# Products of halves for the gate and the squares, later distance tables, and GpSimd's low halves in pieces of 256 columns, in a hybrid decoder layer

## The chip, the cores and the metric

The kernel runs on one core of a Trainium2 chip. The metric is the device time of one execution in microseconds; the median of three runs is given for the kernel before, and beside it one profiled execution whose trace is read here. Engines are named TensorE (PE in the rows, PEld for its weight loads), VectorE (DVE), ScalarE (ACT), GpSimd (POOL) and SyncE (SP).

## The reference

One residual layer over 512 tokens of width 1024, all in float32. What matters, cut down:

```python
h = rmsnorm(x, norm_mix_pre)
p_rwkv, p_conv, p_attn, p_gate = split(h @ w_in)          # 1024 -> 8704 columns
# branch A, RWKV-7 time mixing, 8 heads of 64 (inputs shifted by a token and mixed)
w_log = -softplus(-(w0 + tanh(wl) @ w_up)) - 0.5
a = sigmoid(a0 + al @ a_up)
g = sigmoid(gl) @ g_up                                    # the gate product
kk = k * k_k;  kk = kk * rsqrt(max(sum(kk * kk), 1e-12))  # the sum of squares, by head
state = state * w + (state @ -kk) * (kk * a) + v * k;  y = state @ r
y = groupnorm(y) * ln_w + ln_b + sum(r * k * r_k) * v;  y_a = y * g
# branch B, gated convolution of 3 taps: y_b = b * conv3(c * xc)
# branch C, attention: 3 groups of 4 heads, (window, dilation) = (128, 1), (512, 4), (2048, 16),
# scores + ALiBi distance bias, masked, softmax, groups merged by their denominators: y_c
merged = sum_i sigmoid(gate_i) * (y_i @ w_branch_i)
x = x + rmsnorm(merged @ w_out, norm_mix_post)
x = x + rmsnorm((silu(gate) * up) @ w_ffn_out, norm_ffn_post)    # gate, up = split(rmsnorm(x) @ w_ffn_in)
```

## The kernel before

**Halves.** Nearly every matrix product is made as three products of fp32r operands. ScalarE copies a raw fp32 tile to an fp32r one (the high half), another engine subtracts it from the raw tile (the low half), and TensorE adds high x high, high x low and low x high in PSUM (`three`, L2144). Weights come in slots of 128 x 2048 raw elements, two buffers by turns: SyncE loads `w_raw`, ScalarE makes `w_hi` (`high`, L886), GpSimd makes `w_lo` (`low`, L736, four parts of 512 columns, each announced by itself on `lo_ready`), TensorE waits for each part before it uses it (`part_ready`).

**Stages, in order of the profile's time.** To 87 us the projection columns of the recurrence. From 87 to 424 us four turns `rwkv(T)` of 128 tokens each, in which TensorE fills every stretch between the recurrence's small products with products of the remaining projection (`fill`, `fill_steps`, L2278), written out by hand with a fixed count at each place. From 424 to 487 us the attention, with the last projection slots as fill (`fill_left`, L2462). Then the branch products (to 553), the output projection (to 575), the turn to the FFN input (to 590), six plain FFN slots (to 655), sixteen slots of mixed products (to 811) and the FFN output.

**Recurrence.** In each turn ScalarE takes tanh and sigmoid of the LoRA inputs for the next turn (`lora_inputs`, L997), and later squares `kk` (L1006), then sigmoid of `sig` (L1008), the copy of the gate (L1011), the square root of the sums (L1016), in turns two to four the next slot's `w_hi` (`next_high`), and the exponentials (L1021). TensorE multiplies the gate (`gate`, L2299, fp32) and the squares with a matrix of ones by head (L2316, fp32). VectorE waits for that (L1611). At the end of a turn VectorE normalises y (L1723 to L1744), multiplies by the gate (L1746), and TensorE turns the result (`turn_y`, L2420), asks for the next turn's LoRA products (L2293) and the next gate. In the first turn the turn of y comes after the gate.

**Attention.** Units u = 0 to 7 are heads: 0 to 3 of the window group, 4 to 7 of both dilated groups together. Pairs p are two units. TensorE: `turn_values` (L2472), `scores` (L2488), `turn_probs` (L2497), `outputs` (L2522). VectorE's order: `dilated_bias` (distances from GpSimd's `step_i`, L1509 to L1514, then eight bias tables, L1518), `keep_values` (L1757), `softmax_input` for pairs 0 and 1 (L1781), four low halves (L1800), and so on. For units 4 to 7 the blocks of the 16-dilated group are turned by VectorE in quarters of 32 (`turn_quarters`, L1809) and the others by TensorE. `scores(1)` waits until VectorE has read the scores of pair 0, `turn_probs(4)` until the last values are kept.

**Mixed FFN products.** For each slot s: VectorE adds blocks of raw weights (L2007, L2009, L2013, L2020), ScalarE makes high halves, GpSimd makes the low halves of two blocks at once, 1024 columns in one instruction (`b_low`, L835, and `t12_low`, L842), VectorE those of other blocks (L2025; in the first two slots L2031 too). TensorE's order is p1(s+1), q5(s+1), c12(s), u3(s), c11(s+1), u2, each of twelve products of 256 columns (L2692 to L2694); p1 waits for `b_low`, q5 for `t12_low`.

## Time and profile before

| | |
|---|---|
| median of 3 runs | 943.91 us (943.84 to 943.98) |
| the profiled execution's own time | 944.08 us |
| its span | 942.1 us |
| mean granted TensorE clock | 0.999 |
| TensorE busy | 932.1 us, 6650 products |
| VectorE busy | 647.7 us |
| ScalarE busy | 430.9 us |
| GpSimd busy | 442.9 us |

Products overlap: one with 512 columns is recorded as some 0.39 us long, but the next starts 0.23 us after it. So pitches, start to start, are read and not durations. "Idle before, releaser" names what an engine waited for; x4 with one duration are four instructions in a row, from the first's start to the last's end, which holds waits between them too, and also what an instruction itself waited after its start.

### The profile page before, as it was taken

How to read it: one execution, taken by the hardware profiler on the slowest of the kernel's cores; microseconds unless marked ns; L12 is line 12 of the kernel's file. 1: busy time of each engine (PE TensorE's matmuls, PEld its weight loads, DVE VectorE, ACT ScalarE, POOL GpSimd, SP SyncE). 2: the span in 40 equal slices, each digit the busy share in tenths (PEclk: the TensorE clock that was granted, in tenths of full speed). 3: DMA queues.
4: the chain of work that ended last, by engine and by line, in shares of the span. 5: the costliest groups of instructions: out<-in, count | busy, mean ns of one | idle time of the engine just before them, and what ended most of it. 6: DMA issues, size and time to landing. Idle time of an engine off the chain costs nothing.

```text
span 942.1 us, 16109 instructions
## 1 busy us (share of the span) xinstructions
PE 932.1 (99%) x6650; PEld 786.1 (83%) x6650; DVE 647.7 (69%) x831; ACT 430.9 (46%) x626; POOL 442.9 (47%) x328
## 2 busy tenths in 40 slices
PE   9999999999999999999999999999999999999997
PEld 7888877787887778777778888888999999988886
DVE  6777967766586756899885656988998898411114
ACT  6423515723461462336653425574556655322332
POOL 4884524344253245253245553514765565555551
PEclk9999999999999999999999999999999999999999
DMA  8323332342333265229144842286557666343312
GB/s 290 114 91 112 111 113 92 113 150 73 129 108 130 84 219 183 92 76 327 68 158 158 309 144 71 79 194 162 131 143 176 154 148 169 81 145 112 111 45 89
DMA packets 110805, 128.44 MB, mean 136 GB/s; under 512 B 3216, under 2 KB 87184, under 8 KB 110736
## 3 DMA queue, kind: packets, MB, share of 16 engines
q1 hardware_dynamic: 100224, 102.64, 33.8%
q0 software_dynamic: 2880, 10.49, 5.9%
q10 hardware_dynamic: 7632, 14.32, 4.0%
q8 instruction: 52, 0.85, 0.4%
q14 instruction: 17, 0.14, 0.1%
HBM read 100.70 MB, written 16.25 MB: 124 GB/s over the span
## 4 chain that ended last, share of the span: by engine, by line
PE 52%; issue 26%; POOL 16%; DVE 4%; ACT 1%; DMA 0%; POOLq 0%; DVEq 0%; ACTq 0%
POOL w_lo L741 15%; PE ps L2146 11%; PE ps L2147 11%; PE ps L2148 11%; PE ps L2692 5%; PE ps L2694 5%; PE ps L2693 5%; PE ps L2462 2%; PE ps L2522 1%; DVE x_ct L1527 1%; DVE bias_dil L1518 1%; PE ps L2497 0%; PE ps L2191 0%; PE ps L2488 0%; ACT p_buf L1125 0%
## 5 line engine op out<-in xcount | busy, mean ns | idle before, releaser
L741 POOL TENSOR_TENSOR w_lo<-w_raw,w_hi 128x512 fp32r<-128x512 f32 x220 | 317.6, 1473 | 377.8 <-ACT w_hi L890 377.4
L890 ACT CAST w_hi<-w_raw 128x2048 fp32r<-128x2048 f32 x55 | 105.0, 1909 | 135.4 <-PE ps L2148 110.3
L2278 PE MATMUL ps<-a_hi,w_hi 128*128 128x512 f32 x384 | 154.8, 403 | 0.0
L2278 PE MATMUL ps<-a_lo,w_hi 128*128 128x512 f32 x384 | 152.1, 396 | 0.0
L2278 PE MATMUL ps<-a_hi,w_lo 128*128 128x512 f32 x384 | 151.1, 393 | 0.0
L2278 PEld LDWEIGHTS ps<-a_hi,w_hi 128*128 128x128 f32 x384 | 72.1, 188 | 17.1 <-issue 1.0
L2278 PEld LDWEIGHTS ps<-a_lo,w_hi 128*128 128x128 f32 x384 | 72.2, 188 | 15.5 <-issue 1.0
L2278 PEld LDWEIGHTS ps<-a_hi,w_lo 128*128 128x128 f32 x384 | 72.1, 188 | 15.0 <-ACT xs L1051 0.2
L2063 DVE TENSOR_TENSOR f_lo<-f_all,f_hi 128x1024 fp32r<-128x1024 f32 x11 | 16.1, 1467 | 82.8 <-ACT f_hi L1325 82.8
L2692 PE MATMUL ps<-form_hi,w_hi 128*128 128x256 f32 x256 | 72.5, 283 | 0.0
L2694 PE MATMUL ps<-form_hi,w_lo 128*128 128x256 f32 x256 | 72.5, 283 | 0.0
L2693 PE MATMUL ps<-form_lo,w_hi 128*128 128x256 f32 x256 | 72.5, 283 | 0.0
L2146 PE MATMUL ps<-w_hi,f_hi 128*128 128x512 f32 x176 | 68.6, 390 | 0.0
L2147 PE MATMUL ps<-w_lo,f_hi 128*128 128x512 f32 x176 | 68.5, 389 | 0.0
L2148 PE MATMUL ps<-w_hi,f_lo 128*128 128x512 f32 x176 | 68.5, 389 | 0.0
L981 ACT COPY spill_buf<-ps 128x512 f32<-128x512 f32 x36 | 20.9, 585 | 72.3 <-PE ps L2278 72.0
L835 POOL TENSOR_TENSOR w_lo<-w_raw,w_hi 128x1024 fp32r<-128x1024 f32 x16 | 41.7, 2608 | 24.3 <-ACT w_hi L1253 24.3
L2146 PE MATMUL ps<-a_hi,w_hi 128*128 128x512 f32 (+1 forms) x144 | 53.0, 368 | 0.0
L2147 PE MATMUL ps<-a_lo,w_hi 128*128 128x512 f32 (+1 forms) x144 | 52.7, 366 | 0.0
L2148 PE MATMUL ps<-a_hi,w_lo 128*128 128x512 f32 (+1 forms) x144 | 52.7, 366 | 0.0
L2694 PE MATMUL ps<-form_hi,late_lo 128*128 128x256 f32 x180 | 51.0, 283 | 0.0
L2693 PE MATMUL ps<-form_lo,late_hi 128*128 128x256 f32 x180 | 51.0, 283 | 0.0
(407 smaller groups left out, 2241.6 us busy)
## 6 DMA issues: line engine op xcount, KB each, us to landing
w_raw<-w_in SPq DMA_DIRECT2D x32, 1024.0 KB, 5.2
w_raw<-w_ffn_in SPq DMA_DIRECT2D x44, 512.0 KB, 5.0
spill<-spill_buf ACTq DMA_DIRECT2D x27, 512.0 KB, 3.1
w_raw<-w_ffn_out SPq DMA_DIRECT2D x11, 1024.0 KB, 4.9
late_lo<-w_raw POOLq DMA_DIRECT2D x14, 512.0 KB, 4.6
w_raw<-w_branch SPq DMA_DIRECT2D x5, 1024.0 KB, 8.1
g_ab<-spill SPq DMA_DIRECT2D x8, 512.0 KB, 4.8
w_raw<-w_out SPq DMA_DIRECT2D x4, 1024.0 KB, 7.3
```

The lines of the kernel that those rows point to most:

```text
L741: g.tensor_tensor(w_lo[:, b, c], w_raw[:, b, c], w_hi[:, b, c].bitcast(F), ALU.subtract).then_inc(lo_ready, 1)
L835: g.tensor_tensor(w_lo[:, b, 0:2 * BLK], w_raw[:, b, 0:2 * BLK], w_hi[:, b, 0:2 * BLK].bitcast(F), ALU.subtract).then_inc(b_lo_made.sem, 1)
L890: s.copy(w_hi[:, b], w_raw[:, b]).then_inc(hi_ready, 1)
L981: s.copy(spill_buf[:, b, half], ps[:, 6 + half]).then_inc(spill_copied, 1)
L2146: t_.matmul(dst, w0, a0, start=first, stop=False)
L2147: t_.matmul(dst, w0, a1, start=False, stop=False)
L2148: return t_.matmul(dst, w1, a0, start=False, stop=last)
L2278: last = t_.matmul(ps[:, 6 + half], w[:, kt, half * P:(half + 1) * P], a, start=(kt == 0 and step == 0), stop=(kt == KT - 1 and step == 2))
L2462: last = t_.matmul(ps[:, LEFT_BANK[i]], w[:, kt, half * P:(half + 1) * P], a, start=(kt == 0 and step == 0), stop=(kt == KT - 1 and step = ...
L2692: t_.matmul(dst, hi[:, c], form_hi[f][:, k], start=first and k == 0, stop=False, skip_group_check=not first)
L2693: t_.matmul(dst, hi[:, c], form_lo[f][:, k], start=False, stop=False, skip_group_check=not first)
L2694: last = t_.matmul(dst, lo[:, c], form_hi[f][:, k], start=False, stop=k == KT // 2 - 1, skip_group_check=not first)
```

## The change

It does five things.

1. The gate product is made of halves: ScalarE copies `g_up` once and the sigmoid of each turn to fp32r, VectorE subtracts (`g_up_lo` once, `gate_low` each turn; for turns two to four ahead of the last product of the turn before), TensorE makes three fp32r products.
2. The sum of squares is made of two products of fp32r (the ones are exact): a copy on ScalarE right behind Square and ahead of the sigmoid, a subtraction on VectorE behind the additions to `sig`. In the first turn the first tile's evacuation goes ahead of the sigmoid.
3. GpSimd's low halves in `low`, `b_low` and `t12_low` are made in instructions of 256 columns. What is announced, and when, stays.
4. VectorE's attention order: it waits for the last turn of y, clears `pt_dil`, makes the distances, then four low halves, then values and softmax inputs of pairs 0 and 1, and only then the bias tables.
5. Unit 5's blocks of the 16-dilated group are turned by TensorE (four more) and copied by ScalarE (1024 columns instead of 512), and not by VectorE in quarters.

```diff
+    POOL_PIECE = 256
...
+        ON_VECTOR = (4, 6, 7)
+        def turned_blocks(u):
+            return [b for b in blocks(u // HG) if u not in ON_VECTOR or b[2] == 1]
...
+            def pieces(c0, c1):
+                return [slice(c, c + POOL_PIECE) for c in range(c0, c1, POOL_PIECE)]
             def low(n, b):
                 pool.wait_ge(hi_ready, n + 1)
                 for q in range(LO_PARTS):
-                    c = slice(q * SLOT // LO_PARTS, (q + 1) * SLOT // LO_PARTS)
-                    g.tensor_tensor(w_lo[:, b, c], w_raw[:, b, c], w_hi[:, b, c].bitcast(F), ALU.subtract).then_inc(lo_ready, 1)
+                    for c in pieces(q * SLOT // LO_PARTS, (q + 1) * SLOT // LO_PARTS):
+                        last = g.tensor_tensor(w_lo[:, b, c], w_raw[:, b, c], w_hi[:, b, c].bitcast(F), ALU.subtract)
+                    last.then_inc(lo_ready, 1)
...
             for n in range(5, N_RWKV + 2):
+                if n == N_RWKV:
+                    act.wait_ge(ups_ready, 48)
+                    s.copy(g_up_hi[:], g_up[:]).then_inc(ups_ready, 1)
                 high(n, raw_value(n), n % 2)
...
-                    s.activation(xm[:, RT - 1], xm[:, RT - 1], ACT.Sigmoid).then_inc(gate_ready.sem, 1)
+                    s.activation(xm[:, RT - 1], xm[:, RT - 1], ACT.Sigmoid).then_inc(gate_then_hi.sem, 1)
+                    act.wait_ge(gate_then_hi.sem, gate_then_hi.at(turn))
+                    s.copy(gate_hi[:], xm[:, RT - 1]).then_inc(gate_then_hi.sem, 1)
...
-                s.activation(sq[:], kk[:], ACT.Square).then_inc(sq_ready.sem, 1)
-                need(z_ready)
+                s.activation(sq[:], kk[:], ACT.Square).then_inc(sq_then_hi.sem, 1)
+                need(sq_then_hi)
+                s.copy(sq_hi[:], sq[:].rearrange("p j t -> p (j t)")).then_inc(sq_then_hi.sem, 1)
+                if T == 0:
+                    copy_tile(0)
+                need(z_then_sq_lo)
                 s.activation(sig[:], sig[:], ACT.Sigmoid).then_inc(sig_ready.sem, 1)
...
+            def gate_low(turn):
+                dve.wait_ge(gate_then_hi.sem, gate_then_hi.at(turn, 1))
+                v.tensor_tensor(gate_lo[:], xm[:, RT - 1], gate_hi[:].bitcast(F), ALU.subtract).then_inc(gate_lo_made.sem, 1)
...
+                if T == 0:
+                    dve.wait_ge(ups_ready, 49)
+                    v.tensor_tensor(g_up_lo[:], g_up[:], g_up_hi[:].bitcast(F), ALU.subtract).then_inc(ups_ready, 1)
+                    gate_low(0)
                 need(z_done)
...
+                need(sq_then_hi, 1)
+                v.tensor_tensor(sq_lo[:], sq[:].rearrange("p j t -> p (j t)"), sq_hi[:].bitcast(F),
+                                ALU.subtract).then_inc(z_then_sq_lo.sem, 1)
                 need(ssq_done)
...
                 link(v.tensor_tensor(y1[:], y1[:], y2[:], ALU.add))
+                if T < NT - 1:
+                    gate_low(T + 1)
                 need(g_ready)
...
-            dilated_bias()
+            dve.wait_ge(y_turned.sem, y_turned.at(NT - 1))
+            v.memset(pt_dil[:], 0.0).then_inc(dil_turned.sem, 1)
+            dilated_distances()
+            low_parts(0, NJ)
             keep_values(0, 4)
             softmax_input(0)
             softmax_input(1)
-            low_parts(0, NJ)
+            dilated_bias()
             keep_output(0)
-            v.memset(pt_dil[:], 0.0).then_inc(dil_turned.sem, 1)
             keep_values(2, 4)
             softmax_input(2)
             keep_output(1)
             turn_quarters(4)
-            turn_quarters(5)
...
-                    pe.wait_ge(gate_ready.sem, gate_ready.at(turn))
-                    t_.matmul(ps[:, 2], xm[:, RT - 1], g_up[:], start=True, stop=True).then_inc(g_done.sem, 1)
+                    pe.wait_ge(gate_then_hi.sem, gate_then_hi.at(turn, 1))
+                    pe.wait_ge(ups_ready, 49)
+                    t_.matmul(ps[:, 2], gate_hi[:], g_up_hi[:], start=True, stop=False)
+                    pe.wait_ge(ups_ready, 50)
+                    t_.matmul(ps[:, 2], gate_hi[:], g_up_lo[:], start=False, stop=False)
+                    pe.wait_ge(gate_lo_made.sem, gate_lo_made.base + turn + 1)
+                    t_.matmul(ps[:, 2], gate_lo[:], g_up_hi[:], start=False, stop=True).then_inc(g_done.sem, 1)
...
-                need(sq_ready)
-                t_.matmul(ps[:, 3], head_ones[:], sq[:].rearrange("p j t -> p (j t)"), start=True, stop=True).then_inc(ssq_done.sem, 1)
+                need(sq_then_hi, 1)
+                t_.matmul(ps[:, 3], head_ones[:].bitcast(R), sq_hi[:], start=True, stop=False)
+                need(z_then_sq_lo, 1)
+                t_.matmul(ps[:, 3], head_ones[:].bitcast(R), sq_lo[:], start=False, stop=True).then_inc(ssq_done.sem, 1)
```

`b_low` and `t12_low` are split in the same way, four pieces for one instruction. Semaphores are renamed where they now count two events, and a few tiles are placed anew.

## Rows read from the trace of the kernel before

**Rows 1.** The page's first part: busy us, share of the span, instructions.
```profile
PE 932.1 (99%) x6650; PEld 786.1 (83%) x6650; DVE 647.7 (69%) x831; ACT 430.9 (46%) x626; POOL 442.9 (47%) x328
```
**Rows 2.** TensorE's waits: waiting <- waited for: us in total, times, longest.
```profile
PE ps L2488 <- DVE p_buf L1781: 1.2, 1, 1.2
PE ps L2497 <- DVE proj L1757: 0.8, 1, 0.8
PE ps L2692 <- DVE up L2051: 0.4, 1, 0.4
...
PE ps L2472 <- DMA proj<-spill: 0.2, 1, 0.2
```
**Rows 3.** TensorE's timeline, third turn: start us, us, engine, line, operation, count.
```profile
248.82 1.13 PE L2299 MATMUL ps<-g_up,xm 128*128 128x512 f32 x2
249.78 0.60 PE L2305 MATMUL ps<-ident,xm 128*128 128x128 f32 x4
...
259.32 1.02 PE L2316 MATMUL ps<-sq,head_ones 128*128 128x512 f32 x2
...
260.41 0.40 PE L2278 MATMUL ps<-a_lo,w_hi 128*128 128x512 f32 x1
...
267.02 0.39 PE L2278 MATMUL ps<-a_hi,w_hi 128*128 128x512 f32 x1
267.25 0.39 PE L2278 MATMUL ps<-a_lo,w_hi 128*128 128x512 f32 x1
```
**Rows 4.** Timeline, third turn: VectorE's last product, TensorE's turn of y, ScalarE.
```profile
246.29 0.69 DVE L1746 TENSOR_TENSOR y<-y,g_tok 128x512 f32<-128x512 f32 x1
...
247.20 0.60 PE L2420 MATMUL ps<-ident,y 128*128 128x128 f32 x4
...
257.04 0.65 ACT L1006 ACTIVATE sq<-kk 128x512 f32<-128x512 f32 x1
...
259.68 1.28 ACT L1016 ACT_TABLE_LOAD   x1
261.10 0.63 ACT L1016 ACTIVATE sq<-sq 128x512 f32<-128x512 f32 x1
```
**Rows 5.** Timeline: GpSimd's low halves at three places; TensorE in the output projection.
```profile
5.12 0.73 POOL L749 TENSOR_TENSOR w_lo<-w_raw,w_hi 128x256 fp32r<-128x256 f32 x1 [4.59 <-ACT w_hi L929]
...
263.61 5.99 POOL L741 TENSOR_TENSOR w_lo<-w_raw,w_hi 128x512 fp32r<-128x512 f32 x4 [9.97 <-ACT w_hi L890]
...
564.03 5.03 POOL L741 TENSOR_TENSOR w_lo<-w_raw,w_hi 128x512 fp32r<-128x512 f32 x4 [2.58 <-ACT w_hi L890]
...
569.27 0.40 PE L2146 MATMUL ps<-w_hi,a_hi 128*128 128x512 f32 x1
```
**Rows 6.** Timeline, mixed products, second slot: GpSimd, VectorE, TensorE.
```profile
656.16 2.41 POOL L835 TENSOR_TENSOR w_lo<-w_raw,w_hi 128x1024 fp32r<-128x1024 f32 x1 [5.67 <-ACT w_hi L1253]
658.53 2.85 POOL L842 TENSOR_TENSOR w_lo<-t_second,w_hi 128x1024 fp32r<-128x1024 f32 x1
...
656.72 2.40 DVE L1971 TENSOR_TENSOR f_all<-f_all,f_silu 128x512 f32<-128x512 f32 x1 [0.45 <-ACT f_silu L1220]
659.15 3.31 DVE L2031 TENSOR_TENSOR late_lo<-w_raw,late_hi 128x1024 fp32r<-128x1024 f32 x1
...
661.97 0.28 PE L2692 MATMUL ps<-form_hi,w_hi 128*128 128x256 f32 x1
```
**Rows 7.** Timeline, end of the last turn and attention: VectorE, TensorE.
```profile
421.57 1.67 DVE L1746 TENSOR_TENSOR y<-y,g_tok 128x512 f32<-128x512 f32 x1
...
428.32 5.13 DVE L1518 SCALAR_TENSOR_TENSOR bias_dil<-step_f,ahead_f 128x128 f32<-128x128 f32 x4
...
434.29 1.29 DVE L1757 COPY proj<-ps 128x512 f32<-128x512 f32 x2
...
459.61 1.25 DVE L1809 STREAM_TRANSPOSE pt_dil<-p_buf 32x128 f32<-32x128 f32 x4 [0.18 <-ACT p_buf L1125]
...
437.75 1.79 PE L2488 MATMUL ps<-proj 64*128 64x128 f32 x16 [1.23 <-DVE p_buf L1781]
```

More of the change, by code:

```diff
@@ L834, in b_low @@
                 pool.wait_ge(b_hi_made.sem, b_hi_made.base + s + 1)
-                g.tensor_tensor(w_lo[:, b, 0:2 * BLK], w_raw[:, b, 0:2 * BLK], w_hi[:, b, 0:2 * BLK].bitcast(F),
-                                ALU.subtract).then_inc(b_lo_made.sem, 1)
+                for c in pieces(0, 2 * BLK):
+                    last = g.tensor_tensor(w_lo[:, b, c], w_raw[:, b, c], w_hi[:, b, c].bitcast(F), ALU.subtract)
+                last.then_inc(b_lo_made.sem, 1)
             def t12_low(s):
@@ L841, in t12_low @@
                 pool.wait_ge(t12_hi_made.sem, t12_hi_made.base + s + 1)
-                g.tensor_tensor(w_lo[:, b, 2 * BLK:], t12_of(s)[:], w_hi[:, b, 2 * BLK:].bitcast(F),
-                                ALU.subtract).then_inc(t12_lo_made.sem, 1)
+                for c in pieces(0, 2 * BLK):
+                    to = slice(2 * BLK + c.start, 2 * BLK + c.stop)
+                    last = g.tensor_tensor(w_lo[:, b, to], t12_of(s)[:, c], w_hi[:, b, to].bitcast(F), ALU.subtract)
+                last.then_inc(t12_lo_made.sem, 1)
             def late_low(s):
@@ L1018, in rwkv @@
                     next_high(T - 1, PER_T - 1)
[L1019 removed]
+                    evacuate(0)
                 need(sums_run)
@@ L2515, in outputs @@
                 if kind == 1:
-                    pe.wait_ge(dil_turned.sem, dil_turned.base + 2 * p - 1)
+                    pe.wait_ge(dil_turned.sem, dil_turned.base + 1 + sum(u < 2 * p + 2 for u in ON_VECTOR))
                 bl = blocks(kind)
```

57 lines of the change are left out of this document (31 added, 26 removed).

## The prediction

> **What bounds the kernel now.** I read the page's busy shares first: TensorE is busy for 932.1 of 942.1 us, VectorE and GpSimd for 69% and 47% [rows 1]. So the end is set by the sum of TensorE's instruction pitches and its few gaps. The table of waits comes second: TensorE's named waits are 1.2 us for the score tiles that VectorE reads out, 0.8 us for attention values that VectorE keeps, 0.4 us in the mixed FFN products and 0.2 us for a DMA [rows 2]. Two things can therefore move the time: what TensorE issues, and whether a producer (GpSimd's low halves, ScalarE's high halves, VectorE) that now arrives in time comes late. For the second I took, in the timeline, each producer's end beside the product that needs it.
>
> **Recurrence, products.** Per turn the gate product (L2299) and the sum of squares (L2316) are fp32 with 512 columns, each run as two instructions. Gate: from 248.82 to the next product at 249.78, 0.96 us, of which I put 0.10 down to the change of operand shape after the LoRA products, which stays (the sum of squares, without it, has 0.86). A product of halves is issued every 0.23 us (267.02 to 267.25), so three cost 0.68: 0.18 saved. Sum of squares: from 259.32 to the second fill product at 260.41 is 1.09 us, less that fill product's own 0.23, so 0.86; two products of halves cost 0.45: 0.41 saved [rows 3]. Four turns: 4 x (0.18 + 0.41) = 2.36 us. Bounds: the gate could save 0.28 in three turns (+0.3), or the two extra waits between its three products could cost 0.1 each turn (-0.4).
> The trace shows an fp32 product as two instructions. The Trainium skill, "FP8 and Floating Point Precision", section TensorE Precision Notes, speaks of four passes for true fp32; at 0.23 us a pass the saving would be 0.23 + 0.45 a turn, 2.7 us in all. The rows give less, and I go by them.
>
> **Recurrence, new work.** On VectorE the gate's low half (128x128, 0.25 to 0.3 us) stands ahead of the last product with the gate. That product ends at 246.98 and TensorE turns its result at 247.20, its normal pitch, so nearly nothing covers it [rows 4]: 0.2 us lost in turns two and three, -0.4. In the first turn TensorE asks for the gate before the turn of y, and the low half would be there about when its third product is: -0.05. Its high half follows ScalarE's sigmoid directly and is there before VectorE comes to it. The sum of squares' low half: Square starts at 257.04 and takes 0.65, the copy some 0.6 and VectorE's subtraction 0.69, to 259.1; the second product wants it at 259.5. Covered by 0.3 us.
> The copy of the squares' high half is queued ahead of sigmoid, gate copies, table load, square root and the next high half of the weights on ScalarE. In turns three and four the table load ends at 260.96 and the root starts at 261.10, so the root, the weights' high half behind it and GpSimd's low half at 263.61 slip by 0.5 us [rows 4, 5]. TensorE is 0.41 earlier there. GpSimd's four parts, 5.99 us for all, end at 265.1 to 269.6; TensorE takes the first at 267.02 [rows 3] and then one in six products, 1.36 us: 1.2 to 1.9 us in hand, 0.2 less by the weight loads that go ahead. Less 0.5, 0.41 and the 0.56 of the pieces (below) leaves nothing in the last part, but 0.95 of the 5.99 is waiting for VectorE (5.99 - 4 x 1.26), and VectorE's last two-input operation before its reciprocal moves out from under it. I take 0, with 0.5 a turn as the bad end.
>
> **GpSimd's pieces.** Free of VectorE, four parts of 512 take 5.03 us (1.26 each) and a piece of 256 alone took 0.73 (0.70 in a row, as an estimate, since operations that follow one another overlap by 0.03): a part grows by 0.14 us, a slot by 0.56, 1024 columns by 0.4 [rows 5]. What VectorE gains shows at the same place as what GpSimd loses. A VectorE operation with two SBUF inputs that meets a GpSimd one waits until that ends and then holds it off: VectorE's L1971 took 2.40 instead of 0.69 beside GpSimd's L835, and the next GpSimd operation took 2.85 instead of 2.41 [rows 6]. With pieces VectorE waits 0.7 at most, but can hold GpSimd off after each of them, by 0.45 us per 512 columns.
> The Trainium skill states such a lock (SBUF — State Buffer, section Who interferes with whom: held for the whole instruction, against a GpSimd operation that reads SBUF); the trace agrees, and by it pieces help VectorE and never GpSimd.
> Output projection: the slot whose parts GpSimd makes from 564.03 to 569.06 gives its last part just as TensorE wants it, with the weight load ahead of its product at 569.27 [rows 5]. Four parts 0.14 longer: -0.56. The other slots have 0.9 us or more in hand.
> Mixed FFN products, second set: GpSimd runs 656.16 to 658.57 and 658.53 to 661.38, and TensorE's product with this result starts at 661.97, 0.5 us in hand. In pieces: the first four end at 659.4 (wanted at 660.5). Then VectorE's L2031, 1024 columns, waiting since 658.9 instead of 659.15, takes the port for 1.0 us (now it gets it at 661.38, when GpSimd is done, and ends at 662.46) [rows 6]. Its next two operations, now at 662.7 and 663.4, come to lie beside the last four pieces: 659.4 + 1.0 + 4 x 0.70 + 2 x 0.45 = 664.1 us. So TensorE stops for 2.3 us (0.6 if the long operation stays behind GpSimd). Its gap later in these products (0.4 us of wait [rows 2], 0.56 with the pitch), behind a VectorE chain that GpSimd held up, goes: -1.75 net.
>
> **Attention.** (a) VectorE's last product with the gate in turn four, like the two before it, took 1.67 us instead of 0.69 beside GpSimd [rows 7]. In pieces each takes some 1.15, the attention loads that wait for it start 1.4 us earlier, and the DMA wait (0.2 [rows 2], 0.33 with the pitch) goes: +0.33. (b) The eight bias operations (from 428.32, 5.13 for the first four, to 434.26) leave the path to the first scores, four low halves come onto it. They start at 428.5 and each meets a piece: 4 x 1.15, to 433.0. Keeping the values and the first softmax input then take the same 3.4 us (434.29 to 437.7), to 436.4; TensorE now goes on at 437.75 after 1.23 us of wait, so it wants them at 436.5: +1.2 [rows 7]. Ends: 0 (low halves at 1.7 each) and 1.39. The bias tables then lie beside TensorE's outputs, some 2 us, needed 5 us later. (c) Without the quarters of unit 5 (1.25 us) the values are kept from 460.2, when their turn lands, not from 460.9 [rows 7]: the wait of 0.8 [rows 2], 0.94 with the pitch, shrinks by 0.74. (d) Unit 5 gives TensorE four more turns; four turns of y take up to 0.60 [rows 4], 0.44 by pitch. ScalarE's copy doubles to about 1.0, -0.08 for the outputs behind it. Sum: 0.33 + 1.2 + 0.74 - 0.44 - 0.08 = +1.75.
>
> **The sum.** 2.36 - 0.45 + 1.75 - 0.56 - 1.75 = 1.35 us gained. The profiled execution took 944.08 us (span 942.1 and 2.0 around it), 0.17 above the median of 943.91. That gives 942.7 by the profile's own time, 942.6 by the median's. I predict 942.6.
>
> **The rivals.** (1) The stop in the mixed products doesn't come: the long low half gets the port only after the last piece, or lies elsewhere. For it: the order at a boundary is seen at only a few places. Against it: VectorE had the port at the end of every GpSimd operation that it waited for. The gap at 671 goes all the same, so 2.3 us more are gained, less 0.2: 940.5. (2) The change doesn't take the wait for the first scores away, since the tables' six small operations are still ahead of the low halves and these wait for full pieces: 1.2 us less, and 0.4 to 0.7 more if the values are late too: 944.0 to 944.5. For it: GpSimd is busy there from 428.1 on. (3) Slower: in each later turn the first slot's low half comes late, behind ScalarE's new copy, since VectorE takes the port after most pieces. It decides from the point where the port is lost at two to three more boundaries than I counted: 0.45 us each, in three turns, is 1.35 per boundary; four of them cost 5.4 us: 948.0. Against it: VectorE's reciprocal, 3.4 us with one input, lies in just that stretch.
> The Trainium skill's rule on the lock, as cited above, leaves it to whoever comes first, so it excludes neither (1) nor (3).
>
> **How the numbers follow.** About 0.2% (1.9 us) is what a measurement of this kernel can tell from no change. Forecast 0.46, of which 0.10 lies below 942.0; (1) 0.25; (2) 0.17; (3) 0.12, slower. So faster 0.35, same 0.53, slower 0.12. The range takes in (1) and (2), and leaves out (3) and the outer ends of the bounds: 940.3 to 944.9.
>
> **What would show it.** In the changed kernel's trace: gate 0.7 us and sum of squares 0.45 us in TensorE's timeline; no named wait above 0.3 us for the first scores or the kept values; two gaps that are not there now, some 0.5 us at 569 and 1 to 2.5 us at 662 (less what was gained by then), both for a GpSimd low half; VectorE's 2.4 to 3.3 us operations in the mixed products down to 1.2 to 2. I am wrong if GpSimd's 256 column pieces take more than 0.75 us free of VectorE, or if a TensorE wait for a low half shows in the recurrence.

## The result

The changed kernel takes 948.96 us (median of 6 runs, 946.97 to 950.06) against 943.88 us for the kernel before in the same session (943.32 to 944.01). The ratio is 1.0051, with a 95% interval of 1.0041 to 1.0061: slower by 0.5%, where 942.6 us was forecast, with a range up to 944.9. The scatter grew as well, from 0.7 to 3.1 us. The profiled execution of the changed kernel took 947.77 us (span 946.0), 3.7 us more than the profiled one of before and 1.2 us less than its own median.

The page's first part of the changed kernel, the answer to [rows 1]:

```profile
PE 933.6 (99%) x6658; PEld 787.6 (83%) x6658; DVE 598.2 (63%) x836; ACT 436.5 (46%) x635; POOL 527.7 (56%) x644
```

VectorE is busy for 49 us less and GpSimd for 85 us more; TensorE, which sets the end, got nothing of the first. A stop is, here and below, a time in which TensorE runs no product. Its waits, the answer to [rows 2]:

```profile
PE ps L2744 <- POOL w_lo L860: 2.5, 1, 2.5
PE ps L2250 <- DVE all_ones L1450: 1.2, 1, 1.2
PE ps L2420 <- issue: 0.8, 1, 0.8
PE ps L2540 <- DVE p_buf L1825: 0.6, 1, 0.6
PE ps L2191 <- POOL w_lo L755: 0.5, 2, 0.3
PE ps L2323 <- POOL w_lo L755: 0.3, 2, 0.2
```

The first is the stop that the prediction put into the mixed FFN products. The waits for the score tiles and for the kept values shrank or went (1.2 to 0.6, 0.8 to none). New are a wait for "issue" in the recurrence's small products, and waits for GpSimd's low halves in four more places.

I then set the start of each TensorE product beside the start of the same product before. The difference between the two profiled executions changes at these places (own working from the two traces; plus is time lost):

| place | forecast | measured |
|---|---|---|
| products of halves in four turns, with the gate's low half | -1.91 | -1.60 |
| last parts of the first slot, turns three and four | 0 | +0.85 |
| stop for "issue" in the third turn | - | +1.17 |
| attention: loads -0.26, first scores -0.68, kept values -0.71, transposes +0.43 | -1.75 | -1.22 |
| output projection, one slot | +0.56 | +0.44 |
| plain FFN products: later parts +0.84, turn of x -0.25 | - | +0.59 |
| mixed products: the stop | +2.3 | +2.86 |
| mixed products: half clock behind the stop | - | +1.43 |
| mixed products: the gap ten us later goes | -0.56 | -0.56 |
| sum | -1.35 | +3.96 (span: +3.9) |

Two more differences cancel and have no row: after its first 10 us the changed kernel's profiled execution is 0.5 us ahead, where those of all these kernels differ by up to 0.6, and at 43 us, in the projection, it loses 0.5 us again.

The stop in the mixed products, in the timeline of GpSimd, VectorE and TensorE; compare [rows 6]:

```profile
656.39 3.30 POOL L851 TENSOR_TENSOR w_lo<-w_raw,w_hi 128x256 fp32r<-128x256 f32 x4 [2.93 <-ACT w_hi L1280]
659.64 5.21 POOL L860 TENSOR_TENSOR w_lo<-t_second,w_hi 128x256 fp32r<-128x256 f32 x4
...
659.15 1.61 DVE L2076 TENSOR_TENSOR late_lo<-w_raw,late_hi 128x1024 fp32r<-128x1024 f32 x1 [1.47 <-ACT late_hi L1299]
...
662.02 1.11 DVE L2054 TENSOR_TENSOR t_raw<-t_raw,w_raw 128x512 f32<-128x512 f32 x1
663.05 1.21 DVE L2058 TENSOR_TENSOR w_raw<-w_raw 128x512 f32<-128x512 f32 x1
664.19 1.21 DVE L2065 TENSOR_TENSOR t_raw<-t_raw,w_raw 128x512 f32<-128x512 f32 x1
...
662.08 0.28 PE L2746 MATMUL ps<-form_hi,w_lo 128*128 128x256 f32 x1
664.90 0.38 PE L2744 MATMUL ps<-form_hi,w_hi 128*128 128x256 f32 x1 [2.54 <-POOL w_lo L860]
```

Two engines take turns here. Of VectorE's two-input operations the multiplication with `f_silu` took 2.40 us before and takes 0.73 now, `late_lo` took 3.31 and takes 1.61, and each of the two additions at 664.04 and 666.86 of before took 2.90 and takes 1.21. GpSimd's four pieces take 5.21 us where one instruction took 2.85 [rows 6]: the first waits for `late_lo`, and VectorE comes in between any two of the others (they start at 661.33, 662.54 and 663.68, VectorE's operations at 662.02, 663.05 and 664.19). GpSimd ends at 664.85 (forecast: 664.1), and TensorE, which wanted the result at 662.2, starts again at 664.90. What came behind it stands in the table by stretches of the changed kernel (us, busy of TensorE, its weight loads, VectorE, ScalarE, GpSimd, then TensorE's granted clock, DMA share, GB/s):

```profile
662.00:664.00 2.00, 0.36 (x4) 0.16 (x2) 1.98 (x2) 1.60 (x3) 2.00 (x3) 1.00 0.91 254
664.00:666.00 2.00, 1.10 (x9) 1.10 (x10) 2.00 (x3) 0.66 (x1) 2.00 (x3) 1.00 0.98 261
666.00:667.00 1.00, 1.00 (x8) 1.00 (x8) 0.54 (x1) 0.27 (x1) 1.00 (x1) 0.67 0.02 7
667.00:668.00 1.00, 1.00 (x7) 1.00 (x7) 0.00 (x0) 0.11 (x1) 1.00 (x3) 0.50 0.00 0
668.00:669.00 1.00, 1.00 (x6) 1.00 (x6) 0.00 (x0) 0.00 (x0) 1.00 (x2) 0.50 0.00 0
669.00:670.00 1.00, 1.00 (x8) 1.00 (x7) 0.42 (x1) 0.00 (x0) 1.00 (x3) 0.62 0.00 0
```

The last column but two falls from 1.00 (2.4 GHz) to 0.50 (1.2 GHz) from 666.3 to 669.8. It was at 1.00 all through the stop and fell only 1.4 us after TensorE had started again. TensorE is busy all the time, but issues its 256-column products every 0.21 us instead of every 0.12. That is the 1.43 us which no term of the prediction had.

### The profile page after: what moved, and what is told of

It reads as the page before. It is cut to its first block, busy times and chain, and to the rows that moved or that the text cites. A ratio compares the mean times of both kernels' runs of the same rounds, so it can differ in the third digit from the quotient of the medians.

```text
span 946.0 us, 16459 instructions
## 1 busy us (share of the span) xinstructions
PE 933.6 (99%) x6658; PEld 787.6 (83%) x6658; DVE 598.2 (63%) x836; ACT 436.5 (46%) x635; POOL 527.7 (56%) x644
## 4 chain that ended last, share of the span: by engine, by line
PE 35%; POOL 31%; issue 29%; DMA 2%; DVE 1%; ACT 1%; SPq 1%; POOLq 0%; DVEq 0%; ACTq 0%
POOL w_lo L755 28%; PE ps L2191 6%; PE ps L2193 6%; PE ps L2192 6%; PE ps L2744 6%; PE ps L2746 5%; PE ps L2745 5%; DMA w_raw<-w_in 1%; DMA w_lo<-w_raw 1%; POOL w_lo L860 1%; DVE x L1966 1%; ACT w_hi L908 0%; POOL wide_mask L803 0%; POOL w_lo L851 0%; PE ps L2236 0%
## 5 line engine op out<-in xcount | busy, mean ns | idle before, releaser
L755 POOL TENSOR_TENSOR w_lo<-w_raw,w_hi 128x256 fp32r<-128x256 f32 x440 | 367.0, 869 | 333.7 <-ACT w_hi L908 333.2
L851 POOL TENSOR_TENSOR w_lo<-w_raw,w_hi 128x256 fp32r<-128x256 f32 x64 | 64.5, 1035 | 17.5 <-ACT w_hi L1280 17.3
L2744 PEld LDWEIGHTS ps<-form_hi,w_hi 128*128 128x128 f32 x256 | 49.1, 192 | 2.8 <-POOL w_lo L860 2.7
```

What stands on the lines that cost most here:

```text
L755: last = g.tensor_tensor(w_lo[:, b, c], w_raw[:, b, c], w_hi[:, b, c].bitcast(F), ALU.subtract)
L851: last = g.tensor_tensor(w_lo[:, b, c], w_raw[:, b, c], w_hi[:, b, c].bitcast(F), ALU.subtract)
L2744: t_.matmul(dst, hi[:, c], form_hi[f][:, k], start=first and k == 0, stop=False, skip_group_check=not first)
```

## The experiments

All times are medians; the kernel before had 943.81 to 943.91 us in these sessions.

**Are the pieces the cost, and where?** In `e1_whole` all of GpSimd's low halves are whole again, in `e1_second_whole` only the two of the stop, in `e1_one_whole` only the second of these; `e1_pieces_alone` is the kernel before with the pieces and nothing else.

```diff
-            b_low(1)
-            t12_low(1)
+            b_low(1, 2 * BLK)        # e1_second_whole; e1_one_whole: b_low(1)
+            t12_low(1, 2 * BLK)      # width of a piece, else POOL_PIECE
```

> The changed kernel with GpSimd's low halves in whole instructions again (512, 1024 and 1024 columns); everything else of the change stays. Theory A (the pieces cost the time: VectorE takes the port at most boundaries between two pieces, each time GpSimd's work moves out by about 0.45 us, and where TensorE wants the result it stops): the stop of 2.7 us at 662 goes, the stretch at half clock behind it goes (1.4 us), so do 0.4 us in the output projection, 0.7 us in the plain FFN products and 0.6 us in the recurrence; the gap of 0.56 us at 671 comes back and the first scores wait up to 0.5 us longer. Against before only the recurrence products (-1.9) and the attention (-1.2, less 0.5) are left: 941.3, between 940.8 and 942.5. Theory B (the changed order on VectorE and ScalarE makes TensorE's producers late, whatever the width): the stops stay, 947 to 949.

> The changed kernel, with only the two low halves of the second set of the mixed FFN products whole (two instructions instead of eight); all others stay in pieces. Theory A: the stop of 2.7 us and the 1.4 us of half clock behind it are one thing with one place, so both go and the gap of 0.56 us at 671 may come back: 948.96 - 2.7 - 0.2 - 1.4 + 0.5 = 945.2 (944.6 to 946). Theory A2 (the loss in these products comes from all sets in pieces, the first is just where it shows): the stop moves to a later set and most of it stays, 947 to 949.

> The changed kernel with a single low half whole: the second one of the second set (one instruction of 1024 columns instead of four of 256). The low half ahead of it stays in pieces and ends at 659.7, some 0.9 us later than whole, and VectorE's long low half takes the port there. Theory A: the whole one then runs from about 660.2 to 663, TensorE stops for 0.7 to 1.1 us. If the half clock needs the long stop, it stays away: 948.96 - 2.7 + 0.9 - 1.4 = 945.8. If any stop in these products brings it, 947.2.

> The kernel before with nothing but GpSimd's low halves in pieces of 256 columns. Theory A: all losses come with the pieces alone: stop and half clock 2.7 + 1.4, output projection 0.4, plain FFN 0.7, recurrence up to 0.6 (nothing new is ahead of it on ScalarE here, so perhaps 0), less 0.6 for the gap at 671 and 0.3 to 0.6 in the attention: 943.9 + 4.2 = 948.1 (947 to 949.3). Theory B (it takes the changed order as well): under 945.5.

Measured: 944.52 (ratio 1.0007, interval 0.9998 to 1.0016), 945.42 (1.0014, 1.0005 to 1.0023), 945.31 (1.0016, 1.0007 to 1.0025) and 950.37 (1.0066, 1.0052 to 1.0079).

The two small edits did what theory A says: two instructions in place of eight, at one place, are worth 3.5 us (948.96 to 945.42): the stop and the half clock, less 0.4 us. The gap at 671 of the kernel before did not come back; one of the same kind, for a VectorE result, stands at 684 instead (0.34 us of wait). With one of them whole a stop of 0.7 us is left, as forecast, and the clock stays up. The pieces alone are slower than the whole change, so what they cost isn't made by the new order of the work (theory B); where its 2.3 us beyond my 948.1 come from isn't shown. The profiled execution is the longest of five and 4.1 us over their median (954.42), so its trace says little of the median. It has a stop of 3.8 us at 667, for ScalarE, which itself waits 5.4 us for a result of VectorE (`f_gate`) that stands behind six two-input operations beside pieces.

`e1_whole` is 3.2 us above its expectation. Its waits, and the stretches behind the first scores:

```profile
PE ps L2536 <- DVE p_buf L1821: 2.0, 1, 2.0
...
PE ps L2406 <- DVE wt L1717: 1.0, 1, 1.0
PE ps L2416 <- issue: 0.5, 1, 0.5
```

```profile
438.00:439.00 1.00, 0.60 (x8) 0.58 (x10) 0.96 (x3) 0.00 (x0) 0.00 (x0) 1.00 1.05 387
...
440.00:441.00 1.00, 1.00 (x5) 0.50 (x2) 0.97 (x3) 1.00 (x5) 0.00 (x0) 0.50 1.04 376
...
442.00:443.00 1.00, 1.00 (x4) 0.81 (x3) 1.00 (x3) 1.00 (x6) 0.00 (x0) 0.50 1.06 391
```

Without pieces the first scores wait 2.0 us, longer than before the change, and in this execution the clock falls behind this stop too (1.5 us lost). It is the longest of the eleven (946.01) and lies by these 1.5 us above the median: four executions with a mean granted clock of 0.996 or 0.997 took 945.2 to 946.0 us, the other seven, at 0.998 to 1.000, took 943.7 to 944.6. So in the median the half clock has no part; the longer wait itself, the 1.0 us for VectorE in the fourth turn and the wait for "issue" (both below) do. The cause of the longer wait is the four low halves that the change put ahead of the kept values. VectorE's rows, first of the changed kernel, then of the one with whole instructions; compare the bias operations in [rows 7]:

```profile
429.19 2.27 DVE L1844 TENSOR_TENSOR ya_lo<-y_a,ya_hi_pair 128x512 fp32r<-128x512 f32 x2
431.39 1.21 DVE L1844 TENSOR_TENSOR ya_lo<-y_a,ya_hi_next 128x512 fp32r<-128x512 f32 x1
432.52 1.21 DVE L1844 TENSOR_TENSOR ya_lo<-y_a,ya_hi_last 128x512 fp32r<-128x512 f32 x1
433.76 1.29 DVE L1801 COPY proj<-ps 128x512 f32<-128x512 f32 x2
```

```profile
428.17 3.37 DVE L1840 TENSOR_TENSOR ya_lo<-y_a,ya_hi_pair 128x512 fp32r<-128x512 f32 x2
431.46 1.75 DVE L1840 TENSOR_TENSOR ya_lo<-y_a,ya_hi_next 128x512 fp32r<-128x512 f32 x1
433.13 1.77 DVE L1840 TENSOR_TENSOR ya_lo<-y_a,ya_hi_last 128x512 fp32r<-128x512 f32 x1
434.93 1.29 DVE L1797 COPY proj<-ps 128x512 f32<-128x512 f32 x2
```

With pieces the four take 4.5 us, with whole instructions 6.7. So at this one place, where VectorE is on the path and GpSimd isn't, pieces earn 2.2 us of VectorE's time, and the new order needs them. The old order gets nothing from them: in `e1_pieces_alone` the eight bias operations, which now meet eight pieces and not four parts, take 6.0 us as before, and the first scores wait 2.0 us.

**Each part alone, and pieces only where VectorE is on the path.** `e2_products` and `e2_attention` add one part each to the kernel before. `e2_att_pieces` has both parts, and pieces in the first two slots of attention alone:

```diff
+            for b in range(2):
+                low(S_REST // 2 * 2 + 2 + b, b, POOL_PIECE)
-            with pool.Fori(S_REST // 2 + 1, (S_FIN + 1) // 2, 1) as i:
+            with pool.Fori(S_REST // 2 + 2, (S_FIN + 1) // 2, 1) as i:
```

> The changed kernel with all GpSimd low halves whole, but for the two slots at the start of attention, which stay in pieces of 256. Theory A: the only place where pieces help is here, because VectorE's four low halves are on the path to the first scores: its wait was 2.0 us with whole parts and 0.6 with pieces. TensorE's clock fell for 3.4 us right behind the 2.0 us stop (1.7 us lost), and behind a stop of 0.6 us it stays up. So against the all-whole version (944.5) it gains 1.4 + 1.7: 941.4 (941 to 942). Rival: the half clock after the first scores isn't tied to that stop, 943.1.

> The kernel before with nothing but the gate and sum-of-squares products of halves in the recurrence. By the terms of the prediction alone 943.9 - 2.36 + 0.45 = 942.0. Theory F adds the stop in the third turn: 942.8. What it shows besides: whether a turn's first slot comes late with the new copy on ScalarE alone, without pieces (0.3 us in turns three and four with both); theory A says no.

> The kernel before with nothing but the later distance tables and unit 5's quarters on TensorE. By the prediction alone, with whole instructions on GpSimd (four low halves at 1.7 us on the path instead of the bias): the first scores wait as long as before (0 gained), kept values 0.74 gained, transposes 0.44 lost: 943.6. Theory A (as the all-whole version showed): the wait grows to 2.0 us and the clock falls behind it: 943.9 + 0.8 + 1.7 - 0.7 + 0.4 = 946.1, or 944.4 if the stop is a little shorter and the clock stays.

Measured: 942.15 (ratio 0.9984, interval 0.9975 to 0.9993), 943.81 (0.9999, 0.9990 to 1.0008) and 944.84 (1.0014, 1.0005 to 1.0023).

- The products alone gain nearly what was forecast for them in each turn (0.39 to 0.42 us for the squares, 0.13 to 0.16 for the gate), and lose most of it again: 0.60 us in the stop for "issue", 0.15 for the gate's low half at the end of the second turn and again of the third, and 1.0 us in the fourth, where one of VectorE's operations with two inputs (L1696, 1.39 us instead of 0.48) now meets a GpSimd part and TensorE waits for it (L2406). In the changed kernel, with pieces in the recurrence, 0.1 us is lost there. In `e2_gate_back` (below), which has whole instructions, nothing is. That it depends on how two chains happen to lie beside each other is my reading, and no run moved them on purpose.
- No first slot comes late in the profiles of `e2_products` and `e1_pieces_alone`. So the 0.85 us of the changed kernel need both: ScalarE's new copy ahead of the weights' high half, and the pieces. In its fourth turn the high half starts at 347.54 instead of 346.60, and the eight pieces take 6.78 us instead of 6.00; each alone fits into the 1.2 to 1.9 us in hand.
- The attention part alone loses: the first scores wait 1.7 us (1.2 before), and in the profiled execution the clock stays at 1.00. Of the eleven executions six have a mean granted clock of 0.999 or 1.000 and took 944.4 to 944.8 us; five have 0.996 to 0.998 and took 945.1 to 946.3. So both of my values were right in part: 944.4 for those that stayed at full clock, and up to 1.5 us more for the others, of which there is no profile, but whose clock suggests that it fell.
- With pieces at this place alone the first scores wait 0.2 us and the clock stays up. Against `e1_whole` this place is worth 2.4 us (944.52 to 942.15). The time is 0.7 us above the expectation; two named waits of its trace are the 1.0 us for VectorE in the fourth turn and 0.5 us for "issue".

**The stop for "issue".** In the changed kernel 31 of 32 small products are issued within 0.5 us, and the last comes 1.06 us later:

```profile
307.20 0.70 PE L2431 MATMUL ps<-wt,qb 64*32 64x32 f32 x32
307.82 0.69 PE L2420 MATMUL ps<-state,ar 64*64 64x64 f32 x31
309.36 0.27 PE L2420 MATMUL ps<-state,ar 64*64 64x64 f32 x1 [0.84 <-issue]
309.55 0.50 PE L2323 MATMUL ps<-a_hi,w_hi 128*128 128x512 f32 x1
```

No semaphore is named. In the trace's DMA records a transfer of the instruction queue (16,384 bytes, 52 of them in the run; TensorE's 13,316 products and weight loads make 256 for each) begins shortly before. I compared its start with the product behind the gap:

```
kernel            transfer starts   next product   between
changed                    306.89         309.36      2.47
the same, 2nd profile      307.31         309.69      2.39
e1_whole                   305.68         308.17      2.48
e1_second_whole            309.46         311.96      2.50
e1_one_whole               308.82         311.31      2.49
e2_att_pieces              305.08         307.49      2.41
e2_products                305.26         307.88      2.61
```

The gap is always ahead of the 32nd product of the same burst, whatever the producers do. It looks like waiting for code. In the kernel before the transfer starts at 307.22 and the 32nd product at 309.01, 1.79 us later; 2.5 us after the transfer's start, at 309.7, TensorE is in products of 512 columns, and no gap shows. The change puts one weight load and one product more per gate on TensorE's list, six instructions by this point. `e2_gate_back` makes the gate one fp32 product again; `e3_list_less` keeps the products of halves and leaves out two of ten warm-up products at the very start (eight instructions); `e3_list_more` adds twelve instructions to the kernel before, at its start.

```diff
-            for _ in range(N_WARM):
+            for _ in range(N_WARM - 2):      # e3_list_less
                 t_.matmul(ps[:, 7, 0:P], all_ones[:], all_ones[:], start=True, stop=True)
+            for _ in range(3):               # e3_list_more
+                t_.matmul(ps[:, 7, 0:8], all_ones[:], all_ones[:, 0:8], start=True, stop=True)
```

> As the run before it, and the gate product is one fp32 product again (no high and low halves of gate and gate weights on ScalarE and VectorE); the sum of squares stays in halves. Theory F (instruction loading): the stop of 0.7 to 1.1 us inside the small products of the third turn, at a fixed distance of 2.49 us behind the start of a 16 KB instruction transfer, comes from the six instructions more on TensorE's list by that point, which move the border of the loaded block into a burst of fast products; without them it goes. Sum: +0.7 to 1.1 for the stop, +0.4 for the low half ahead of the last product with the gate, +0.2 where VectorE's chain in the third and fourth turns came late, -0.7 for four gate products: 0.6 to 1.0 faster than the run before it, 940.6. Rival (the stop has to do with producers, not with the list): the stop stays and it is 0.1 to 0.3 slower, or as fast.

> The version with products of halves, the attention change and pieces in attention alone (942.15), with eight warm-up products at the start instead of ten: eight instructions fewer on TensorE's list, the gate's six more undone. Theory F: the stop of 0.66 us in the third turn goes, 941.5, if the start is no later (the two products fill time in which TensorE would wait for its first weights). Rival: the stop stays, 942.1.

> The kernel before with three tiny fp32 products (8 columns, 12 instructions on TensorE's list) behind its ten warm-up products at the very start; nothing else. Theory F (the stop in the third turn is the wait for a 16 KB block of instructions, whose border the six to eight extra instructions moved into a burst of small products): the same stop without any edit in the recurrence, 0.4 to 1.1 us near 309, ending 2.49 us behind the start of the instruction transfer; the start itself costs up to 0.3 us. 944.3 to 945.2. Rival (the stop belongs to the gate's new producers): no stop, 943.9 to 944.2.

Measured: 940.93 (ratio 0.9971, interval 0.9960 to 0.9981), 941.72 (0.9977, 0.9968 to 0.9986) and 944.53 (1.0014, 1.0005 to 1.0023).

In both kernels with the shorter list the burst is whole. `e3_list_less`, whose recurrence is that of `e2_att_pieces`:

```profile
306.35 0.69 PE L2430 MATMUL ps<-wt,qb 64*32 64x32 f32 x32
306.97 0.69 PE L2419 MATMUL ps<-state,ar 64*64 64x64 f32 x32
```

An edit 305 us earlier, at the start of the kernel, takes the stop away: it is the place on the list, not a producer. Here the transfer starts at 305.62 and the 32nd product follows it by 1.84 us, without a gap. So it is in all eight kernels in which the traces count six to eight products and weight loads fewer ahead of this one (`before`, `e1_pieces_alone`, `e2_attention`, `e2_gate_back`, `e3_first_slots`, `e3_list_less` and both `e4`): 1.3 to 2.0 us behind the transfer's start, and no stop; in all seven profiles that count as many as the changed kernel it waits for 2.39 to 2.61 us. `e3_list_more` was a miss, and says how narrow the place is: the transfer began at 302.45, 4.8 us earlier than before (307.22), and there was no stop at 309. My reading is that what starts the transfer had moved in front of the slow products, so that the code was there in time; no run tests it. Its time of 944.53 lies in my range for another reason: the profiled execution (943.96) is the shortest and loses nothing (0.06 us gained by the end), seven of the eleven took 944.0 to 944.6 us and four took 946.2 to 946.4, all at a mean granted clock of 0.999. What these four lose, no profile shows. That the transfer is the cause rests on the fixed distance and on the place on the list; the transfer itself wasn't changed. The Trainium skill, "Advanced Engine Details and Errata", section ISA Cache, has a cache line of 16 KB, which is 256 instructions; the trace agrees in both (16,384 bytes a transfer, 256 products and weight loads for each).

`e2_gate_back` is the fastest kernel of this study, 3.0 us faster than the kernel before: its recurrence gains 0.42 to 0.46 us in each of the four turns and has none of the three losses. Its expectation of 0.6 to 1.0 us against `e2_att_pieces` was low (1.2), since the 1.0 us wait for VectorE in the fourth turn went as well.

**The projection, and a second profile.**

> The kernel before with only the first four slots of the projection in pieces (n = 2 to 5). In the profile of the changed kernel these cost 0.4 us between 28 and 46 us, in three other profiled executions with the same slots in pieces 1.5 to 2.8 us, with one slot taking 10.1 us instead of 5.95. Theory A: this place, with no room and VectorE busy with two-input operations, is where the changed kernel's median is worse than its profile and its scatter 3 us wide: 945.4, between 944.3 and 946.5, with a scatter over 1 us. Rival (the scatter comes from elsewhere): 944.3 at most, scatter under 0.8.

> The changed kernel once more, for a second profile. Theory A: the stop at 662 (2.5 to 2.9 us) with half clock behind it, the stop in the third turn (0.7 to 1.2), 0.4 us in the output projection and 0.3 us in the first slot of turns three and four are there again; the projection's first slots lose 0.4 to 2.8 us, and its time goes with that: 947 to 950.

Measured: 944.24 (ratio 1.0004, interval 0.9995 to 1.0013; 943.28 to 945.66) and 948.95 (1.0056, 1.0037 to 1.0074).

GpSimd's rows for one slot of the projection, in the kernel before and in `e3_first_slots`:

```profile
33.84 5.95 POOL L741 TENSOR_TENSOR w_lo<-w_raw,w_hi 128x512 fp32r<-128x512 f32 x4
```

```profile
35.18 10.14 POOL L743 TENSOR_TENSOR w_lo<-w_raw,w_hi 128x256 fp32r<-128x256 f32 x8
```

VectorE makes its own two-input operations beside these parts, and comes in at most borders. In the profiled executions this costs TensorE, at 42 to 46 us, 0.5 and 0.7 us (changed kernel, both profiles) or 1.9 to 2.4 us (`e1_second_whole`, `e1_one_whole`, `e1_pieces_alone`, `e3_first_slots`). The scatter of `e3_first_slots` is 2.4 us, over the 1 us of theory A, but it rests on one execution, the profiled one (945.66): the other nine took 943.28 to 944.68. The median is only 0.4 us above before, as the rival had it, and no more than can be told from no change. So the place can cost 2 us in an execution; that it makes the changed kernel's scatter of 3.1, and the 1.2 us by which its median lies above its profile, isn't shown. The second profile of the changed kernel has every other loss in its place and size: the stop in the mixed products 2.8 us, as in the first by the same measure, half clock for 3.4 us, "issue" 1.1, output projection 0.45, first slots 0.45 each.

**Does a long stop bring the half clock by itself?** In the kernel before, with all instructions whole, the same low half is made twice, all of it in `e4_stop_long` and the first 256 of its 1024 columns in `e4_stop_short`, which delays it:

```diff
+                if again:
+                    link(g.tensor_tensor(w_lo[:, b, 2 * BLK:2 * BLK + again], t12_of(s)[:, 0:again],
+                                         w_hi[:, b, 2 * BLK:2 * BLK + again].bitcast(F), ALU.subtract))
...
-            t12_low(1)
+            t12_low(1, 2 * BLK)      # e4_stop_long; e4_stop_short: BLK // 2
```

> The kernel before, whole instructions, with one low half of the mixed FFN products (second set, second part) made twice: a stop of TensorE on purpose, with no piece anywhere. GpSimd: 658.6 to 661.4, VectorE's long low half takes the port, then 2.4 to 2.9 us more to 664.8 or 665.3; TensorE stops for 2.9 to 3.3 us at 662. Theory C (the half clock follows the length of the stop): the clock falls for 3.4 us behind it as in the changed kernel, 1.4 to 1.7 us lost besides; with the gap at 671 gone (0.5), 943.9 + 3.1 + 1.6 - 0.5 = 948.1. Rival (the half clock has to do with the changed kernel's other edits): 946.5, clock at full speed.

> The same with only 256 columns made twice: 0.73 us, and VectorE's long low half comes in between: the real low half ends at about 663, TensorE stops for 0.8 to 1.4 us. Theory C: stops of 1.0 to 1.7 us left the clock up in the other runs, so it stays up here: 943.9 + 1.1 - 0.5 = 944.5 (944.2 to 945). Rival (any stop in these products, where TensorE's products are short, brings the half clock): 946.

Measured: 947.54 (ratio 1.0040, interval 1.0026 to 1.0055) and 944.61 (1.0007, 0.9998 to 1.0017). The same two stretches of the long and of the short one:

```profile
661.00:664.00 3.00, 0.72 (x7) 0.51 (x5) 3.00 (x3) 1.32 (x2) 2.96 (x1) 1.00 0.12 30
...
666.00:668.00 2.00, 2.00 (x12) 2.00 (x11) 2.00 (x2) 0.38 (x1) 1.03 (x1) 0.50 0.63 160
```

```profile
661.00:664.00 3.00, 2.04 (x17) 1.84 (x17) 2.96 (x2) 1.32 (x2) 2.47 (x2) 1.00 0.70 200
...
666.00:668.00 2.00, 2.00 (x19) 2.00 (x18) 2.00 (x5) 1.78 (x3) 0.65 (x1) 1.00 0.00 0
```

The long stop (2.75 us later than before, 2.6 by the waits) is followed by 3.4 us at half clock, 1.5 us lost; the short one (1.1, 1.0 by the waits) by none. Nothing of the change is in these kernels, so the fall belongs to the stop. Theory C holds for these two lengths. Between them the length doesn't decide alone: behind 2.0 us at the first scores the clock fell in `e1_whole` and stayed at 1.00 in `e1_pieces_alone`, and behind the 1.7 us of `e2_attention` the mean clock of some executions suggests that it fell. Even the changed kernel's shortest execution (946.97) has a mean granted clock of 0.999, in which 3.4 us at half clock have no room (they alone make 0.998). What decides there stays open. Rows of `e1_pieces_alone` behind its stop at the first scores (TensorE starts again at 440.16):

```profile
438.00:440.00 2.00, 0.17 (x1) 0.00 (x0) 2.00 (x4) 0.58 (x1) 0.00 (x0) 1.00 1.04 384
440.00:442.00 2.00, 1.84 (x17) 1.42 (x18) 1.93 (x6) 0.47 (x3) 0.00 (x0) 1.00 1.05 386
442.00:444.00 2.00, 2.00 (x10) 1.60 (x11) 1.97 (x6) 2.00 (x10) 0.00 (x0) 1.00 1.07 392
```

The Trainium skill, "TensorE: Matmul & The Clock Gate", section What's actually happening, has the clock halved when TensorE has been idle, and restored when it has been busy again. The trace agrees in both directions, but the fall comes 0.3 to 1.6 us after TensorE has started again, never in the stop itself.

## Why the prediction was wrong, point by point

The forecast was 1.35 us gained, and the profiled execution lost 3.96. The steps that failed: the mixed products' stop was priced at its own length (1.43 us of half clock came with it, and it was 0.56 longer); the longer instruction list had no term (1.17); the first slots of turns three and four were taken at 0 (0.85); the plain FFN products, whose slots got no sum of their own, lost 0.59; and the attention gained 0.53 less. With the products and their low half (0.31 less) and the output projection (0.12 better) this is the whole difference of 5.3. The median lies another 1.2 us above this execution, and no trace shows where.

- **Products of halves** (2.36 forecast): 0.39 to 0.40 us a turn for the squares and 0.13 to 0.15 for the gate, 2.1 in all. Right. The gate's low half cost 0.12 to 0.13 us at the end of the second and of the third turn, where 0.2 was counted, and smaller slips in the recurrence as much again, so -1.60 net against -1.91.

```profile
248.11 0.50 PE L2345 MATMUL ps<-g_up_hi,gate_hi 128*128 128x512 f32 x1
248.45 0.40 PE L2347 MATMUL ps<-g_up_lo,gate_hi 128*128 128x512 f32 x1
248.68 0.40 PE L2349 MATMUL ps<-g_up_hi,gate_lo 128*128 128x512 f32 x1
248.92 0.49 PE L2355 MATMUL ps<-ident,xm 128*128 128x128 f32 x3
```

  From 248.11 to 248.92 is 0.81 us, against 0.96 in [rows 3].

- **"I take 0, with 0.5 a turn as the bad end"** for the first slot of the later turns: 0.43 us in each of turns three and four. The sum in that paragraph already had nothing left in the last part; the value should have been nearer its bad end. It is also the sign of being wrong that the prediction named, a wait of TensorE for a low half in the recurrence: two of 0.2 us show. ScalarE's high half slipped by 0.94 us in the fourth turn, not by 0.5. This is rival (3)'s place, but with a sixth of its price, and it isn't what made the kernel slower.
- **The instruction list** was in no term. I counted what the added products cost and not that they move the code behind them: 1.17 us, half of what the products gained. Nothing in the rows before showed a stop of this kind, but "+2 instructions per gate" could have been noted as a risk with a bound.
- **Attention** (1.75 forecast, 1.22 measured): the four low halves took 4.5 us (4.6 forecast) and the kept values gained 0.71 (0.74). They began at 429.19, which is 428.8 in the times of before (TensorE was 0.4 us late by then), and not at 428.5. Loads and first scores together gained 0.94, not 0.33 + 1.2. Of the difference 0.18 is a slip in the sum: when the values are there at 436.4, a product that started at 437.75 can gain 1.35 at most, however early the loads are. The size was off, not the step.
- **Output projection**: eight pieces take 5.60 us against 5.03 in [rows 5]. This is 0.57 more, as forecast (0.56), and TensorE lost 0.44.

```profile
563.25 5.60 POOL L755 TENSOR_TENSOR w_lo<-w_raw,w_hi 128x256 fp32r<-128x256 f32 x8 [2.48 <-ACT w_hi L908]
...
568.91 0.50 PE L2191 MATMUL ps<-w_hi,a_hi 128*128 128x512 f32 x1 [0.26 <-POOL w_lo L755]
```

- **Mixed products**: the place and the order in which the engines take the port came out as worked out, and the gap at 671 went. The size was 2.8 us against 2.3 (2.1 by the sum's own times, 664.1 less 661.97). The step that failed is the price: I took a stop of TensorE to cost its own length. It cost 1.43 us more, at half clock.
- **The stages that I didn't look at.** The prediction weighed the pieces at two slots and in the recurrence. "The other slots have 0.9 us or more in hand" held in the output projection, but not elsewhere. In the plain FFN products GpSimd takes 10.12 us for a slot that took 6.58. The two loads that refill its buffer wait for that and are issued at 614.05, not at 610.96, so that they run together with the two low-half transfers of the next slot. These are issued at 613.96 and 615.11 (613.85 and 615.74 before) but take 7.3 and 9.6 us to land, and no longer 5.1 and 5.8, and TensorE waits for them and what follows: 0.84 us.

```profile
603.91 10.12 POOL L755 TENSOR_TENSOR w_lo<-w_raw,w_hi 128x256 fp32r<-128x256 f32 x8 [7.14 <-ACT w_hi L908]
...
624.71 0.50 PE L2191 MATMUL ps<-a_hi,w_hi 128*128 128x512 f32 x1 [0.29 <-DMA w_lo<-w_raw]
```

  In the projection a slot went from 5.95 to 9.4 us (changed kernel) or 10.1 (`e3_first_slots`), with 0.5 to 2.4 us lost. My bound of 0.56 us a slot counted pieces free of VectorE; a contended slot grew by three and a half to four us.
- **The range** left out the bad ends of several terms, though all have one cause, the pieces, and so come together. The half clock and the code were outside of any end. By the medians, the pieces outside attention cost 6.8 us (948.96 to 942.15), where the forecast had them at about 2.3 (0.56 + 1.75). What is left of the change gains 1.8, where the forecast had 3.7 (2.36 - 0.45 + 1.75). Nearly all that is missing there stands in the profile of `e2_att_pieces`: 0.7 us in the stop for "issue" and 1.0 in the wait for VectorE in the fourth turn, two losses for which the prediction had no term. So a sum without the pieces would have been 1.9 us too good as well.

## What to carry to other kernels

Cutting an instruction into pieces so that another engine can come in between is a transfer of time from one engine to the other, at every border; do it only in the stretch where the engine that gains is on the path, and list every slot of the engine that pays (here one place that gained 2.4 us against 6.8 us of loss elsewhere). Cost a stop of TensorE with what follows it: here stops of 1.2 us and less cost their length, those of 2.5 us and more another 1.5 us in every profile, and those between now the one, now the other. And read a profile beside the other executions' times and clocks: three of the profiles here were the longest execution of their kernel, by 1.4 to 4.1 us over the median. And when an edit adds instructions ahead of a burst of very small products, look in the trace for a gap without a semaphore in that burst: a few instructions more or less anywhere before it can bring it or take it away.

## What the runs showed of the hardware

- TensorE's granted clock against its stops (by the named waits): behind stops of 0.6 us (changed kernel, attention), 1.0 (`e4_stop_short`), 1.2 (before), 1.7 (`e2_attention`, profiled execution) and 2.0 (`e1_pieces_alone`, first scores) it stayed at 1.00; behind stops of 2.0 (`e1_whole`), 2.5 (changed kernel, both profiles), 2.6 (`e4_stop_long`) and 3.8 (`e1_pieces_alone`, 667 us) it was at 0.50 for 3.4 us each time. The fall began 1.4 us after TensorE had started again in the changed kernel (664.90 to 666.34) and in `e1_whole`, 1.6 in the second profile, 0.4 in `e4_stop_long` and 0.3 in `e1_pieces_alone`.
- A piece of 256 columns on GpSimd takes 0.73 us and follows the one ahead of it by 0.70; with a VectorE operation of two SBUF inputs waiting at each border it takes 1.2 and follows by 1.13 to 1.21 (changed kernel, 661 to 665 us), and the 512-column VectorE operation takes 1.1 to 1.2 instead of 0.68. In attention 512-column VectorE operations took 1.7 us beside 512-column GpSimd parts, and 1.2 beside pieces.
- From the start of a 16 KB instruction transfer to the first product behind it took 2.39 to 2.61 us in the seven profiles with the stop; the burst of 64-row products issues 31 products and 31 weight loads in half a us and ran into that.
